# Hybrid decoder layer: weight low parts on VectorE, strided low copies on GpSimd, and the value product ahead of the turning of probabilities

## The reference, cut to what matters

```python
h = rmsnorm(x, attn_norm[l])
proj = h @ w_in[l]
qkv_a, b_q, b_k, b_v, m_q = jnp.split(proj, IN_SPLITS, axis=-1)
# A: three groups of 4 heads of 64, window/dilation (128,1), (512,4), (2048,16)
o_a = dilated_mixture_attn(qkv_a, positions, a_q_norm[l], a_k_norm[l])
# B: 8 query heads on 2 key heads, window 128, a sink per head
o_b = sink_swa_gqa(...)
# M: 4 heads of 128 into 256 memory tokens
o_m = memory_attn(...)
```

## Time and profile before

| | us |
|---|---|
| median of 3 runs | 1875.52 |
| lowest and highest | 1873.69, 1876.38 |
| the profiled execution | 1876.01 |
| its span, first to last instruction | 1874.2 |
| TensorE busy in the span | 1777.5 (95%) |
| VectorE, ScalarE, GpSimd busy | 738.5, 577.8, 639.5 |
| mean granted clock of TensorE | 0.976 of full speed |

### The profile page before, as it was taken

How to read it: one execution, slowest core, us unless ns; L and a number is a source line. 1 busy time by engine, 2 the same in 40 slices (tenths; PEclk the granted TensorE clock), 3 DMA queues, 4 the chain that set the end, 5 groups by cost and what they waited for, 6 DMA issues and landing times. The chain is left out here.

```text
span 1874.2 us, 23271 instructions
## 1 busy us (share of the span) xinstructions
PE 1777.5 (95%) x8889; PEld 1443.6 (77%) x8889; DVE 738.5 (39%) x1320; ACT 577.8 (31%) x1059; POOL 639.5 (34%) x535
## 2 busy tenths in 40 slices
PE   4789998989989899999999998999999999999999
PEld 3577787767767778888888886888888888888887
DVE  4634435337885402210055232333423424342343
ACT  4434555534444422322121322311221221122121
POOL 5444545453342122222144632413321331332122
PEclk8899999999989999999999998999999999999999
DMA  5301102011210043332345602202201210220002
GB/s 188 107 17 35 35 2 56 15 34 26 68 35 1 1 116 90 100 103 90 102 157 164 217 1 67 68 23 67 67 22 45 67 45 22 67 67 21 24 23 90
DMA packets 118270, 119.28 MB, mean 64 GB/s; under 512 B 15340, under 2 KB 95916, under 8 KB 118188
## 3 DMA queue, kind: packets, MB, share of 16 engines
q1 hardware_dynamic: 118188, 118.16, 20.6%
HBM read 101.25 MB, written 16.89 MB: 63 GB/s over the span
## 5 line engine op out<-in xcount | busy, mean ns | idle before, releaser
L1890 PE MATMUL ps<-act_hi,f_hi 128*128 128x512 f32 x704 | 278.9, 396 | 6.3 <-DVE f_lo L1655 6.3
L1890 PE MATMUL ps<-act_hi,f_lo 128*128 128x512 f32 x704 | 276.8, 393 | 0.0
L1890 PE MATMUL ps<-act_lo,f_hi 128*128 128x512 f32 x704 | 274.5, 390 | 0.0
L1655 POOL TENSOR_TENSOR f_lo<-ffn_area,f_hi 128x1024 fp32r<-128x1024 f32 x65 | 155.3, 2419 | 87.7 <-ACT f_hi L1736 87.7
L1845 DVE TENSOR_TENSOR attn_out<-ps,attn_out 128x512 f32<-128x512 f32 x160 | 106.5, 687 | 136.4 <-PE ps L1910 136.3
L1890 PEld LDWEIGHTS ps<-act_hi,f_hi 128*128 128x128 f32 x704 | 133.2, 189 | 33.2 <-DVE f_lo L1655 6.7
L1890 PEld LDWEIGHTS ps<-act_hi,f_lo 128*128 128x128 f32 x704 | 132.8, 189 | 31.1
L1890 PEld LDWEIGHTS ps<-act_lo,f_hi 128*128 128x128 f32 x704 | 132.8, 189 | 29.3
L1555 PE MATMUL ps<-act_hi,g_hi 128*128 128x512 f32 x384 | 152.1, 396 | 3.1 <-DVE g_lo L1490 3.1
L1555 PE MATMUL ps<-act_hi,g_lo 128*128 128x512 f32 x384 | 151.2, 394 | 0.0
L1555 PE MATMUL ps<-act_lo,g_hi 128*128 128x512 f32 x384 | 149.9, 390 | 0.0
(11 more groups left out here) (220 smaller groups left out, 3751.9 us busy)
## 6 DMA issues: line engine op xcount, KB each, us to landing
ffn_area<-in_w_up_dram SPq DMA_DIRECT2D x44, 512.0 KB, 4.0
gates<-gate SPq DMA_DIRECT2D x24, 512.0 KB, 3.1
gate<-gates SPq DMA_DIRECT2D x24, 512.0 KB, 3.8
g_raw<-in_w_gate_dram SPq DMA_DIRECT2D x23, 512.0 KB, 4.6
ffn_area<-in_w_down_dram SPq DMA_DIRECT2D x22, 512.0 KB, 3.7
attn_out<-in_x_dram SPq DMA_DIRECT2D x16, 512.0 KB, 5.9
w_raw<-in_w_in_dram SPq DMA_DIRECT2D x16, 384.0 KB, 3.5
attn_out<-in_w_in_dram SPq DMA_DIRECT2D x16, 384.0 KB, 4.2
```

Of the source, the lines that this page charges most:

```text
L1655: eng.tensor_tensor(f_lo[:, b, :], f_raw[b], f_hi[:, b, :].bitcast(F32), ALU.subtract).then_inc(f_lo_done[b], 1)
L1890: ins = pe.matmul(ps[:, 2 * q + half, :], w[:, q, k * P:(k + 1) * P], a[:, k, half * 512:(half + 1) * 512], start=(k == 0 and i == 0), sto ...
```

## The change

It makes three edits, all in `input_projections`:

1. The low parts of weight slices are all made by VectorE, in slice order, each in its step k, from stage memv on; only stage memk keeps even slices on GpSimd. The two semaphores for even and odd slices become one for each engine, and the wait for slice n asks for all of GpSimd's and VectorE's up to n.
2. The low part of the strided activations is copied by GpSimd at the end of its work for the slot, behind `norm_and_rope`, and no longer by VectorE in step 2.
3. For a unit n TensorE does `weigh_values(n - 3)` ahead of `turn_probs(n - 2)`.

```diff
+def low_on_pool(n):
+    return n < 8 and n % 2 == 0
+def low_count(n):
+    on_pool = sum(low_on_pool(m) for m in range(n + 1))
+    return on_pool, n + 1 - on_pool
...
         def w_split(eng, n):
-            eng.wait_ge(w_lo_odd if n % 2 else w_lo_even, n // 2 + 1)
+            on_pool, on_dve = low_count(n)
+            eng.wait_ge(w_lo_pool, on_pool)
+            if on_dve:
+                eng.wait_ge(w_lo_dve, on_dve)
...
         # w_low
-                              ).then_inc(w_lo_odd if n % 2 else w_lo_even, 1)
+                              ).then_inc(w_lo_pool if low_on_pool(n) else w_lo_dve, 1)
...
         # GpSimd
+            def gather_low(j):
+                gather_from(pool, j)
+                pool.tensor_copy(gathered(j)[:, 1], columns(act_lo, j)).then_inc(lo_gathered, 1)
...
                 for n in pair_of(j)[:1]:
                     x_low(pool, n)
-                for s in last_job_of:
-                    if last_job_of[s] == j and s + 1 < len(STAGES):
-                        for k in range(0, 8, 2):
-                            w_low(pool, 8 * (s + 1) + k)
+                if strided(j + 1):
+                    gather_low(j + 1)
...
         # VectorE
-            def gather_low(j):
-                gather_from(dve, j)
-                dve.tensor_copy(gathered(j)[:, 1], columns(act_lo, j)).then_inc(lo_gathered, 1)
...
-                    if k == 2 and strided(j + 1):
-                        gather_low(j + 1)
                     if 0 <= j - 1 < NJ and k == TURN_AT[KIND[j - 1] == "B"]:
                         copy_k(j - 1)
-                    if k % 2 and j in last_job_of.values() and JOBS[j][0] + 1 < len(STAGES):
+                    if j in last_job_of.values() and JOBS[j][0] + 1 < len(STAGES):
                         w_low(dve, 8 * (JOBS[j][0] + 1) + k)
...
         # TensorE
                         score(n)
+                        if n >= 3:
+                            weigh_values(n - 3)
                         if n >= 2:
                             turn_probs(n - 2)
-                        if n >= 3:
-                            weigh_values(n - 3)
                         n += 1
```

More of the change, by code:

```diff
@@ L300, in input_projections @@
         raw_in = [sem(f"raw_in{n}") for n in range(8)]
-        w_hi_done, w_lo_even, w_lo_odd, w_used = (sem(n) for n in ("w_hi_done", "w_lo_even", "w_lo_odd", "w_used"))
+        w_hi_done, w_lo_pool, w_lo_dve, w_used = (sem(n) for n in ("w_hi_done", "w_lo_pool", "w_lo_dve", "w_used"))
         proj_done, sq_done, ss_done, rstd_done, normed, roped = (
```

## The result

The changed kernel takes 1855.97 us (median, 1854.01 to 1857.89), the kernel before 1875.67 beside it: ratio 0.9897, interval 0.9879 to 0.9914, so 19.7 us less. I had forecast 1864.5, in a range from 1856.0 to 1872.0. The profiled execution has a span of 1852.2 us against 1874.2, and all of the 22.0 us lie ahead of the gates: TensorE projects for the last slot's job 22.05 us sooner.

A forecast was written before the change was run, and what follows sets the result against it. The prediction took TensorE as the bound, with the loss in gaps at the changes of stage. Gains of 1.4 (a), 2.4 (b), 0.9 (c), 6.8 (d) and 0 for the rest, 11.5 us, took 1876.0 to 1864.5; range 1856 to 1872.

The forecast's parts named there:

- (d): Slots 27 and 28: earlier low parts and reloads shorten slot 28 by 8.1 us, slot 27 loses 1.3; net gain 6.8.
- (a): Slots 1 and 2: slice 15's low part is no longer held by GpSimd's; gain 1.4 us.
- (b): Slots 3 and 4: scaling of x no longer held, reloads and casts come sooner; gain 2.4 us.
- (c): Slots 11, 12 and 19: no gain in 11 and 19, slot 12 loses its excess; gain 0.9 us.
- G: Length of GpSimd's strided low copy, taken as 2.4 us, between 1.24 and 4.8.
- (e): Slots 35 and 36: VectorE's added low parts against less holding by GpSimd; taken as 0, bounds -1.5 and +3 us.
- Part 2: Strided low copy on GpSimd: at 2.4 us it is hidden within its slot and costs nothing; taken as 0.
- larger gain: Rival, 1857 us: one-input copies don't hold VectorE, minima of slots 11 and 19 come 2.3 us sooner each; chance 0.12.
- The rival on VectorE: 1870 us: VectorE becomes the bound at the changes of stage, its added low parts aren't won back; chance 0.13.
- that on reloads: Rival, 1870 us: the weights' DMAs land late for another reason than their buffers; chance 0.07.
- the one of a late copy: Rival, slower: the copy on GpSimd outlasts its slot, 1888 us if it takes 5.5; chance 0.05.
- Part 3: Values weighed ahead of the turning on TensorE: its waits stay; taken as 0, bounds -1 to +1 us.

The follow-up runs named there:

- e3: The kernel before with only the low parts of the later stages moved to VectorE; 1862.82 us (ratio 0.9930).
- e10: The changed kernel with the low part of stage B's slice 0, in slot 27, on GpSimd again; 1858.70 us (0.9911).
- e2: The changed kernel with the turning of probabilities in front of the weighing again; 1863.76 us (ratio 0.9937).
- e4: The kernel before with only the strided low copy moved to the end of GpSimd's slot; 1883.71 us (ratio 1.0040).
- e11: The changed kernel with the strided low copy made twice on GpSimd, one behind the other; 1863.22 us (0.9927).
- e6: The changed kernel with one more 128x128 transposition of probabilities between score and weighing, for 77 pairs of heads; 1869.16 us.
- e7: The changed kernel with one more 128x128 transposition of probabilities behind the weighing, directly in front of the turning; 1860.15 us.

## Why the prediction was right or wrong

**(d), slots 27 and 28: right, with its mechanism.** Forecast -8.1 and +1.3, measured -8.17 and +1.30; e3 and e10 show the cause. That both figures fit to 0.1 us is in part luck: for slot 27 I had counted a fall of the clock that the changed kernel doesn't have (1.00), and e2, whose clock falls to 0.89 there, has -8.8 and +2.7. Without the swap, which is part of the -8.17, parts 1 and 2 give 6.2 to 6.6 net where I had 6.8.

**(a) and (b): mechanism right, sizes within 1 us, (a)'s not shown.** 1.9 and 1.5 in e2 against 1.4 and 2.4. The last low part of slot 1 ends at 51.49 us, 1.64 sooner, and TensorE turns at 60.67, 1.64 sooner than in the earlier trace rows. But e4, which changes nothing ahead of slot 11, has 1.0 less in slots 0 to 2 as well; kernels with part 1 have 0.8 to 2.2 less there. In slots 3 to 5 the kernels without part 1 have up to 0.5 more, those with it 1.3 to 2.0 less.

**(c): slot 12 right, slots 11 and 19 mis-sized.** Slot 12's excess went: 0.92 without the swap, forecast 0.9. I had slots 11 and 19 at 0. They gave 0.65 and 1.7 in e2, with clocks of 0.91 and 0.90 (0.91 and 0.83 before). I had put the minima at 13.65 us into slot 11, with G counted in full as one turn; they came at 12.9, since the low part was held only until the copy's end, 1.9 us more than alone.

**(e): right within its bounds**, +0.8 in e2 and +0.5 in the changed kernel against 0. The middle of my bounds, -1.5 and +3, was 0.75 and not the 0 that I called it; kernels with the same orders there range from +0.5 to +1.4, nearer to that middle than to 0. The wait that I had named, the copy of k behind slice 6's low part, was there: 2.01 us. Slot 35 itself got 0.4 shorter.

**Part 2: right, but it gains nothing.** G was 2.1 to 2.2 and ended before its slot; e11 bears the slack out. Its price is the hold of VectorE's low part in slots 11 and 19. The Trainium skill (GPSIMD Engine Reference, Performance pitfalls for Q7 kernels) gave an estimate of 2.5; both strides of this kernel ran a little faster, and the measurement decides. That VectorE's two-input low part was held by a GpSimd copy is as the Trainium skill has it (SBUF — State Buffer, Who interferes with whom): a VectorE operation with two inputs in SBUF and a GpSimd one that reads SBUF need the same port pair, and the second to start waits for the first's whole length. The trace agrees with 2.82 against 0.95. With that my rival "larger gain", by which a copy holds nothing, falls. The rival on VectorE was right of slot 35's copy of k only, that on reloads was wrong (e10), and the one of a late copy came true in e4 alone.

**Part 3: wrong, and it is nearly the whole miss of 8.5 us.** I took 0, bounds -1 to +1; it gave 7.8 in the medians, 10.0 by slots. The step that failed is "once or twice in either direction: bounds -1 to +1": I asked only what waits for what, and took for granted that TensorE's own time for three steps doesn't depend on their order. The rows that could have told me were in the trace of before: the projection begins 0.37 us behind the weighing, whose four matmuls stream 512 columns together, while a single projection matmul over 512 columns is followed 0.23 us later (346.47 and 346.70 above). The Trainium skill (TensorEngine Tiling (Array Packing), Key Properties) says that a change of tiling mode drains TensorE, with no figure. The trace agrees that a change costs time, 0.16 us by e6 against e7; that a drain is what takes it no run shows. I had not weighed that page. With one change less for each of two groups in 16 undisturbed A slots, 0.17 x 32 = 5.4 (measured 6.0), and for the 22 groups of slots 29 to 34, 3.7 (measured 2.4, some of these slots being bound by waits), the sum would have stood at 1855.4.

**The range.** That 1856.0 comes as near to the range as it does is luck. The forecast's own range, 1860 to 1869, misses. Its extension down to 1856 was there for the rival "larger gain", whose mechanism didn't come true.

## What to carry to other kernels

When steps are reordered on one engine, count how often the shape of the array's use changes between neighbours, besides asking who waits: here about 0.17 us a change, in nearly every A and B slot, made two fifths of the gain (7.8 of 19.7 us in the medians). Where one engine's late operation frees the first buffer of a queue of loads, that single operation can be worth several us (4.9 in slot 28), and the helper that does it soonest is the right one even if it is the busier. An order on a helper engine is read best from what it does just ahead of the step that TensorE waits for: low parts that waited for casts stood in front of minima that were long ready. By slots that was worth 2.3 us at each of two changes of stage, and nothing at the third.

## What the runs showed of the hardware

- TensorE: 0.15 to 0.18 us for each change among matmuls on 128*128, 64*128 and 128*64 (five orders), also between the last two.
- GpSimd: a strided copy of 128x1024 from f32 to fp32r takes 2.02 to 2.23 us (up to 2.84 beside VectorE's low parts), VectorE's 1.09 to 1.26 where nothing holds it; a stride of 8 tokens costs 0.1 to 0.2 more than one of 4.
- The clock can eat a closed gap: in two kernels with the same orders slot 36 took 17.70 and 16.34 us at granted clocks of 0.81 and 1.00.
